# Routing of a two-layer encoder rebuilt: fewer serial steps, paced list scatters, gains loaded first, attention's projections spread over eight steps

## The chip, the cores and the metric

The kernel runs on one core of a Trainium2 chip. The metric is the device time of one execution in microseconds. A core has five engines with queues of their own: TensorE (PE, its weight loads shown as PEld), VectorE (DVE), ScalarE (ACT), GpSimd (POOL) and SyncE (SP, here only for transfers). Semaphores order them.

## The reference, cut to what matters

```python
# x: 1024 tokens x 1024, float32
h = x
h = h + mixer_ab(rmsnorm(h, g1), ...)       # layer 0: A: 9-chunk attention, 8 heads; B: window attention with sinks
h = h + dense_swiglu(rmsnorm(h, g2), ...)   # 1024 -> 2816 -> 1024
h = h + mixer_c(rmsnorm(h, g1), ...)        # layer 1: gated spatial mixing
h = h + moe_swiglu(rmsnorm(h, g2), ...)
return rmsnorm(h, final_norm)

def moe_swiglu(h, w_router, w_gate_e, w_up_e, w_down_e):
    logits = (xt @ w_router).astype(jnp.float32)      # 8 experts
    top_val, top_idx = lax.top_k(logits, TOP_K)       # TOP_K = 2
    gates = jax.nn.softmax(top_val, axis=-1)
    ...                                               # tokens sorted by expert
    ys = lax.ragged_dot(jax.nn.silu(hg) * hu, w_down_e, sizes)   # 1024 -> 3584 -> 1024
    ys = ys * gates.reshape(-1)[order][:, None].astype(ys.dtype)
    out = jnp.zeros_like(xt).at[tok].add(ys)
```

## The kernel before, in words

**Products.** Every float32 product is made of three products of a high and a low part (`product`, L307 on, all recorded at L316). Weights come in units of 128 x 1024 (512 KB) through four buffers `wraw[0..3]`. SP sends them (`load_units`, L292) when the buffer's last split is done; ACT makes the high part (`hi_part`, L298), DVE the low part (`lo_part`, L302). PE counts finished units in `unit_used`, DVE finished splits in `lo_done`.

**Start** (`start_act`, `start_dve`, `values_pe`). ACT and DVE multiply the first half of x by the gains of the norm and split it; PE multiplies it by the first weights, unscaled, and meanwhile sums squares and spreads the norm's factor (`start_sums_pe` L365, `start_spread_pe` L387). The gains are loaded by POOL, behind its first small operations. PE's first work of all is a small product for the T5 bias table (L2192), which waits for three small loads; its reader `ext_dve` stands behind the second weight part.

**Attention** (`attend_pe`, `attend_act`, `attend_dve`): 4 pairs of heads x 8 tiles t of 128 tokens, 32 steps, software-pipelined by hand. A step of PE: transposes of the A probabilities, A scores of the next step, half of the slices of a half projection if there is one, A values, B transposes, B scores, the other slices, B values. Pair p's second halves (`LATER`) are at t = 0, 1, 2 (units QA, KA, QB), and the first halves of the next pair (`AHEAD`) at t = 4, 5, 6; steps 3 and 7 have none. A half projection is 8 slices of k into one bank; ACT and DVE copy it out (`half_act`, `half_dve`, L784, L789) at the end of the step.

**Routing** (`mix_out_pe`, `route_dve`, `route_pool`). After the last projection of layer 1, PE makes the logits (L1114) and turns the hidden rows (`rows_pe`, L1128), ACT scales and copies them (`row_act`, L1150, L1152), and sends each at once: 16 scaled rows to `xrow_d` and 16 plain ones to `hrow_d`. DVE takes the top 2, sums the assignments of the tiles one after the other (L1647), PE ranks them (L1095 to L1097), DVE finds the least-loaded expert (`least`, `first_ok`), then every token's slot, then 8 masks `mine` (L1700) of the tokens of the first list, which PE turns into indices (`list_pe`, L1135); then the gates and the table of items (`cand`, `items_ok`), with the indices `tokl0` in the middle (L1721). POOL gathers x of the first item by these indices (L1778) once every `xrow_d` write has landed, and then scatters 16 x 128 entries of (token, gate) into the lists `tok_d` (L1787), and clears three buffers.

**Items** (`by_width`, `item_pe`, ...): a list of up to 384 tokens of one expert, at the least width of `WIDTHS` that holds it. 28 gate units and 28 up units, then 28 units of the down product: 84 units, in quads. Here there are 8 items: 3 of width 240, 2 of 256, 2 of 288, 1 of 304. x is turned by `turn_x_pe` (L1839). Beside the first units of an item the rows finished by the item before are normalised (`norm_beside_act`, `norm_beside_dve`). PE, ACT and DVE read the number of items as soon as `items_ok` is there.

A few lines that set the order:

```python
            for c in range(2):
                load_units(sp, src_e(e0, 0, c), Q_MOE, c)          # SP: 4 parts of the first quad, behind first_ok
            ...
            pool.wait_ge(slots_ok, 1)
            pool.wait_ge(gates_ok, 2)
            for t in range(NT):
                for c in range(2):
                    pool.indirect_dma_start(tok_d[:], ...)          # 16 scatters, back to back
```

## Time and profile before

| | |
|---|---|
| median of 3 runs | 3593.17 us (3589.37 to 3595.44) |
| profiled execution | 3593.88 us, its span 3592.1 us |
| mean granted clock of PE | 0.992 |
| DVE, ACT, POOL busy | 50%, 43%, 6% of the span |
| attention (steps) | about 103 to 405 us |
| routing, from the last projection to the first item | 1520.7 to 1556.2 us |
| items | 1556 to 3571 us |

Times in rows are microseconds from the span's start. A row of a timeline has its start, the time from its start to its end, engine, line, operation, written and read names, count, and in brackets the idle time before it and what ended it. A granted clock of 1.00 is 2.4 GHz and 0.50 is 1.2 GHz.

### The profile page before, as it was taken

The numbers are of one execution on the slowest core, as the hardware profiler recorded it, in microseconds if no ns is written. First come the engines' busy times: TensorE is split into PE (matmuls) and PEld (weight loads), VectorE is DVE, ScalarE is ACT, GpSimd is POOL, SyncE is SP. The second block draws the span as 40 slices with busy tenths as digits, with TensorE's granted clock in tenths as the row PEclk, the third lists the DMA queues.
The fourth block names the chain that finished last, engine by engine and source line by source line (L and its number), as shares of the span: only waits on it lengthen the run. The fifth ranks groups of instructions, "written<-read, shape, count | busy, mean of one in ns | idle before, by whom it ended". The sixth has DMA issues, their size and how long they took to land. (4 is left out here: it accounts for less than half of the span.)

```text
span 3592.1 us, 71989 instructions
## 1 busy us (share of the span) xinstructions
PE 3508.3 (98%) x27356; PEld 3338.3 (93%) x27356; DVE 1808.7 (50%) x2607; ACT 1544.6 (43%) x2216; POOL 203.3 (6%) x207
## 2 busy tenths in 40 slices
PE   8999899999999999979999999999999999999997
PEld 7888799999999999879899898998999999999997
DVE  6455543333333554365565555555655545545544
ACT  4455433333333333355454554544544444434433
POOL 1000000000000000040010010100101000000100
PEclk9999999999999999989999999999999999999999
DMA  5111323333322322266565565755656545544543
GB/s 198 35 47 45 138 94 97 96 97 118 97 96 94 123 88 97 81 209 205 186 236 194 193 230 186 234 194 196 228 187 205 182 158 181 191 164 155 183 160 124
DMA packets 158043, 540.81 MB, mean 151 GB/s; under 512 B 23480, under 2 KB 23520, under 8 KB 157920
## 3 DMA queue, kind: packets, MB, share of 16 engines
q1 hardware_dynamic: 129440, 467.72, 39.3%
q0 software_dynamic: 23872, 62.99, 5.0%
q10 hardware_dynamic: 4608, 8.39, 0.6%
q8 instruction: 86, 1.41, 0.2%
q14 instruction: 37, 0.30, 0.0%
HBM read 515.54 MB, written 45.48 MB: 156 GB/s over the span
## 5 line engine op out<-in xcount | busy, mean ns | idle before, releaser
L302 DVE TENSOR_TENSOR wl<-wraw,wh 128x1024 fp32r<-128x1024 f32 x884 | 1082.4, 1225 | 1307.0 <-ACT wh L298 1303.5
L298 ACT ACTIVATE wh<-wraw 128x1024 fp32r<-128x1024 f32 x884 | 934.3, 1058 | 1128.5 <-PE ps L316 1123.0
L316 PE MATMUL ps<-exh,wh 128*128 128x240 f32 (+3 forms) x3588 | 1018.0, 284 | 5.3 <-issue 5.2
L316 PE MATMUL ps<-exl,wh 128*128 128x240 f32 (+3 forms) x3584 | 1017.5, 284 | 1.5 <-issue 1.5
L316 PE MATMUL ps<-exh,wl 128*128 128x240 f32 (+3 forms) x3584 | 1017.2, 284 | 1.5 <-issue 1.4
L316 PE MATMUL ps<-xs,wh 128*128 128x256 f32 x5248 | 819.4, 278 | 2.4 <-DVE qAl L789 2.0
L316 PEld LDWEIGHTS ps<-xs,wh 128*128 128x128 f32 x5248 | 696.5, 188 | 12.5 <-issue 8.5
L316 PEld LDWEIGHTS ps<-exh,wh 128*128 128x128 f32 x3588 | 676.3, 189 | 8.0 <-issue 7.8
L316 PEld LDWEIGHTS ps<-exh,wl 128*128 128x128 f32 x3584 | 675.8, 189 | 1.6 <-issue 1.6
L316 PEld LDWEIGHTS ps<-exl,wh 128*128 128x128 f32 x3584 | 675.8, 189 | 1.6 <-issue 1.4
L316 PE MATMUL ps<-xs,wl 128*128 128x256 f32 x2624 | 512.8, 277 | 0.0
L316 PEld LDWEIGHTS ps<-xs,wl 128*128 128x128 f32 x2624 | 396.6, 188 | 0.0
L316 PE MATMUL ps<-wh,mah 128*128 128x512 f32 (+1 forms) x560 | 221.6, 396 | 0.0
L316 PE MATMUL ps<-wh,mal 128*128 128x512 f32 (+1 forms) x560 | 221.1, 395 | 0.0
L316 PE MATMUL ps<-wl,mah 128*128 128x512 f32 (+1 forms) x560 | 219.6, 392 | 0.0
L1288 ACT ACTIVATE mst<-ps 128x240 f32<-128x240 f32 (+3 forms) x224 | 87.5, 391 | 304.9 <-PE ps L316 230.4
L316 PE MATMUL ps<-mah,wh 128*128 (+2 forms) x672 | 200.3, 298 | 1.0 <-DVE exl L1850 1.0
L316 PE MATMUL ps<-mah,wl 128*128 (+2 forms) x672 | 200.0, 298 | 0.0
L316 PE MATMUL ps<-mal,wh 128*128 (+2 forms) x672 | 200.0, 298 | 0.0
L316 PE MATMUL ps<-ah,wh 128*128 (+2 forms) x704 | 138.3, 278 | 0.0
L316 PE MATMUL ps<-al,wh 128*128 (+1 forms) x704 | 138.1, 278 | 0.0
L316 PE MATMUL ps<-ah,wl 128*128 (+1 forms) x704 | 137.6, 277 | 0.0
(325 smaller groups left out, 3523.2 us busy)
## 6 DMA issues: line engine op xcount, KB each, us to landing
wraw<-in_w_expert SPq DMA_DIRECT2D x676, 512.0 KB
wraw<-in_w_main SPq DMA_DIRECT2D x208, 512.0 KB
hT<-in_xT POOLq DMA_DIRECT2D x2, 2048.0 KB, 9.7
h_d<-hT POOLq DMA_DIRECT2D x2, 2048.0 KB, 10.0
hT<-h_d POOLq DMA_DIRECT2D x2, 2048.0 KB, 13.7
xrow_d<-rows ACTq DMA_DIRECT2D x16, 256.0 KB, 2.0
hrow_d<-rows ACTq DMA_DIRECT2D x16, 256.0 KB, 3.4
yraw<-y_d POOLq DMA_DIRECT2D x4, 768.0 KB, 7.8
```

The costliest lines, as they stand in the source:

```text
L298: act.activation(wh[:, j], wraw[:, j], ACT.Copy).then_inc(hi_done, 1)
L302: dve.tensor_tensor(wl[:, j], wraw[:, j], wh[:, j].bitcast(F32), ALU.subtract).then_inc(lo_done, 1)
L316: mm = pe.matmul(out[:, s], a, b[:, s], start=first and part == 0 and c == 0, stop=last and part == 2 and d == n)
L1288: act.activation(buf[:, par, 0:n], bank(b + par, n), ACT.Silu).then_inc(silu_done, 1)
```

## The change

- **Start:** SP sends the gains ahead of everything. The T5 product goes behind the second slice of the value products, `ext_dve` behind the fourth weight part. The counters of the raw halves are joined with those of the scaled ones.
- **Attention:** a half projection is cut into pieces of 2 to 4 slices, two per step, over all eight steps from t = 3 of one pair to t = 2 of the next; the first pair keeps its halves at t = 0 to 2. At t = 0 (pairs 1 to 3) and t = 4 (pairs 0 to 2) the copies come early in the step.
- **Routing:** no serial sum over tiles: PE adds eight shifted bf16 products. The masks come from the rank among the least-loaded expert alone, ahead of the slots; the slots and gates are computed after the turn of x (`slots_dve`). The item table is smaller (13 items in place of 24). ACT copies a row before it sends the previous one, and only the first 8 plain rows and all scaled rows are sent by ACT; the last 8 plain rows stay in SBUF and POOL sends them one per unit of the first item (`last_rows_pool`); DVE waits for them (`rows_out`) behind the first twelve units. The 16 scatters wait for units 12, 14, ... 42 of the first item. POOL's clears and the final gains come ahead of them. The logits of the second half run one unit earlier. The first quad's part 0 is loaded behind `first_ok`, parts 1 to 3 only when x of the first item has arrived, and split after the turn.
- **Items:** the squares beside an item move two units back. The count of items is read by ACT and DVE after the last item.

```diff
+        THIRDS = ((QA, range(0, 3)), (QA, range(3, 6)), (QA, range(6, 8)), (KA, range(0, 3)),
+                  (KA, range(3, 6)), (KA, range(6, 8)), (QB, range(0, 4)), (QB, range(4, 8)))
+            if p == 0 and t < 3:
+                return (0, 1, *HALVES[2 * t + place])
+            if t < 3:
+                return (p, 1, *THIRDS[2 * t + 2 + place])
+            if p + 1 == PAIRS_A:
+                return None
+            if t < 7:
+                return (p + 1, 0, *THIRDS[2 * (t - 3) + place])
+            return (p + 1, 1, *THIRDS[place])
...
+            if 0 in ks:
+                pe.wait_ge(lo_done, unit_of(p, which) + 1)
+                pe.wait_ge(pj_lo, halves_before(p, half, which))
...
+        def early(p, t):
+
+            return (t == 0 and p >= 1) or (t == 4 and p + 1 < PAIRS_A)
...
+            pe.matmul(bank(SMALL, n, RANK), belowb[:], sentb[:], start=True, stop=False)
+            for back in range(1, NT + 1):
+                m = n - back * NE
+                mm = pe.matmul(bank(SMALL, m, RANK + back * NE), onesb[:], sentb[:, 0:m], start=False, stop=back == NT)
...
+        def last_rows_pool(pool):
+
+            pool.wait_ge(row_cp, 32)
+            for e in range(8):
+                t, b = 4 + e // 2, e % 2
+                pool.wait_ge(unit_used, 4 * Q_MOE + e + 1)
+                pool.dma_start(hrow_d[t * P:t * P + P, 512 * b:512 * b + 512], rows[:, e]).then_inc(last_st, 16)
...
+                    pool.wait_ge(unit_used, 4 * Q_MOE + 12 + 2 * (2 * t + c))
                     pool.indirect_dma_start(tok_d[:], bass.IndirectOffsetOnAxis(ap=slot[:, c, t:t + 1], axis=0),
                                             entry[:, c, t], None).then_inc(tok_st, 16)
...
-            for c in range(2):
-                load_units(sp, src_e(e0, 0, c), Q_MOE, c)
+            for j in range(4):
+                if j == 1:
+                    sp.wait_ge(x_got, 48)
+                sp.wait_ge(lo_done, 4 * Q_MOE + j - 3)
+                sp.dma_start(wraw[:, j], src_e(e0, 0, j // 2)[:, j % 2]).then_inc(raw[j], 16)
...
             turn_x_act(act, 0, XB0)
+            for j in range(1, 4):
+                hi_part(act, Q_MOE, j)
+            gap_exp_act(act)
+            act.wait_ge(items_ok, 1)
...
+            lo_part(dve, Q_MOE, 0)
             turn_x_dve(dve, 0, XB0)
+            for j in range(1, 4):
+                lo_part(dve, Q_MOE, j)
+            slots_dve(dve, own)
+            dve.wait_ge(items_ok, 1)
```

## Rows read from the trace of the kernel before

**Rows 1.** Part 1 of the page: busy us, share of the span, instructions

```profile
PE 3508.3 (98%) x27356; PEld 3338.3 (93%) x27356; DVE 1808.7 (50%) x2607; ACT 1544.6 (43%) x2216; POOL 203.3 (6%) x207
```

**Rows 2.** Waits of PE over the span: us in total, times, longest us

```profile
PE ps L2192 <- DMA onehot<-in_onehot: 10.8, 1, 10.8
...
PE ps L316 <- issue: 8.1, 14, 1.1
```

**Rows 3.** Stretch of the first 5 us: busy us and instructions by engine, clock, DMA share, GB/s

```profile
0.00:5.00 5.00, 0.00 (x0) 0.00 (x0) 0.00 (x0) 1.49 (x2) 3.78 (x13) 1.00 0.57 195
```

**Rows 4.** Timeline of the start: start us, us, engine, line, operation, idle time before and its releaser

```profile
8.04 1.33 ACT L335 ACTIVATE rsh<-yT,gains 128x512 fp32r<-128x512 f32 x2 [5.55 <-DMA gains<-in_gains]
...
12.15 0.80 PE L316 MATMUL ps<-wh,rsh 128*128 128x512 f32 x1
...
30.11 0.88 DVE L381 TENSOR_SCALAR dg<-ident,vstat 128x128 f32<-128x128 f32 x4
...
31.41 1.06 PE L387 MATMUL ps<-dg,ones 128*128 128x128 f32 x8
```

**Rows 5.** Timeline of DVE in attention: the copies of the finished B outputs

```profile
134.26 0.29 DVE L963 COPY ystB<-ps 128x128 f32<-128x128 f32 x1 [2.30 <-PE ps L763]
...
141.49 0.28 DVE L963 COPY ystB<-ps 128x128 f32<-128x128 f32 x1
...
152.58 0.29 DVE L963 COPY ystB<-ps 128x128 f32<-128x128 f32 x1 [2.53 <-PE ps L763]
...
175.62 0.29 DVE L963 COPY ystB<-ps 128x128 f32<-128x128 f32 x1 [2.43 <-PE ps L763]
...
181.44 0.29 DVE L963 COPY ystB<-ps 128x128 f32<-128x128 f32 x1
```

**Rows 6.** Timeline from the ranks to the first item's first product

```profile
1528.67 0.43 PE L1095 MATMUL ps<-sent,below 128*128 128x64 f32 x2 [1.11 <-DVE before L1647]
...
1529.54 0.17 DVE L1669 COPY place<-ps 128x8 f32<-128x8 f32 x1 [0.44 <-PE ps L1097]
...
1532.52 0.69 ACT L1150 ACTIVATE rows<-ps,rstd_t 128x512 f32<-128x512 f32 x1 [0.46 <-ACT rows L1150]
...
1535.89 2.73 DVE L1700 TENSOR_SCALAR mine<-range_c,lowest 128x384 bf16<-128x384 f32 x8
...
1540.30 0.16 DVE L1721 SCALAR_TENSOR_TENSOR tokl<-firstf 128x3 uint32<-128x3 f32 x1
...
1542.14 1.08 POOL L1778 DMA_INDIRECT xg<-xrow_d,tokl  x1 [17.84 <-DMA xrow_d<-rows]
...
1544.84 1.43 POOL L1778 DMA_INDIRECT xg<-xrow_d,tokl  x1 [0.30 <-issue]
...
1551.47 4.46 PE L1839 MATMUL ps<-ident,xg 128*128 128x128 f32 x24 [9.05 <-DMA xg<-xrow_d,tokl]
...
1556.22 0.37 PE L316 MATMUL ps<-exh,wh 128*128 128x240 f32 x1 [0.28 <-issue]
```

**Rows 7.** Part 5 of the page: DVE's split of a weight part

```profile
L302 DVE TENSOR_TENSOR wl<-wraw,wh 128x1024 fp32r<-128x1024 f32 x884 | 1082.4, 1225 | 1307.0 <-ACT wh L298 1303.5
```

**Rows 8.** Two stretches of 5 us in the first item, columns as in rows 3

```profile
1560.00:1565.00 5.00, 2.15 (x11) 1.36 (x9) 0.00 (x0) 0.00 (x0) 3.78 (x5) 1.00 0.02 1
...
1565.00:1570.00 5.00, 2.33 (x8) 1.69 (x8) 0.00 (x0) 0.00 (x0) 3.78 (x4) 0.51 0.02 1
```

**Rows 9.** Timeline: the last scatter, ACT's first and the later items' first Silu

```profile
1570.00 0.97 POOL L1787 DMA_INDIRECT tok_d<-entry,slot  x1 [0.30 <-issue]
...
1573.48 1.28 ACT L1288 ACT_TABLE_LOAD   x1 [16.54 <-remote]
...
1804.58 1.28 ACT L1288 ACT_TABLE_LOAD   x1 [1.63 <-PE ps L316]
...
2036.10 1.28 ACT L1288 ACT_TABLE_LOAD   x1 [1.63 <-PE ps L316]
```

**Rows 10.** Timeline of ACT behind the last item

```profile
3574.91 1.28 ACT L2223 ACT_TABLE_LOAD   x1 [2.27 <-issue]
```

More of the change, by code:

```diff
@@ L607, in values_pe @@
                             mm.then_inc((v_mm, unit_used)[g], 1)
+                        if g == 0 and k == 1:
+                            pe.wait_ge(setup_in, 48)
+                            pe.matmul(bank(6)[0:8, 0:EXT_B], t5s[:], onehot[:], start=True, stop=True).then_inc(t5_mm, 1)
                         if g == 0 and k == 4:
@@ L1092, in mix_out_pe @@
                 if e == 5:
-                    pe.wait_ge(sent_ok, 1)
-                    pe.wait_ge(t_root, 2)
-                    pe.matmul(bank(SMALL, NT * NE, RANK), below[:], sent[:].rearrange("p t e -> p (t e)"), start=True, stop=False)
-                    pe.matmul(bank(SMALL, NT * NE, RANK), ones[:], before[:, 0:NT].rearrange("p t e -> p (t e)"), start=False, stop=True)
-                    pe.matmul(bank(SMALL, NE, COUNT), ones[:], before[:, NT], start=True, stop=True).then_inc(rk_mm, 1)
+                    ranks_pe(pe)
             for e in range(8):
-                if e == 4:
+                if e == 6:
                     list_pe(pe)
@@ L1643, in route_dve @@
             own(last)
+            dve.tensor_tensor(sentb[:, 0:NT * NE], pick[:, 0].rearrange("p t e -> p (t e)"), pick[:, 1].rearrange("p t e -> p (t e)"),
+                              ALU.add).then_inc(sent_ok, 1)
             dve.tensor_tensor(sent[:], pick[:, 0], pick[:, 1], ALU.add)
-            own(dve.memset(before[:, 0], 0.0))
-            for t in range(NT):
-                last = dve.tensor_tensor(before[:, t + 1], before[:, t], sent[:, t], ALU.add)
-                if t < NT - 1:
-                    own(last)
-            last.then_inc(sent_ok, 1)
-            own(dve.tensor_copy(tokb[:].rearrange("p t a -> p (t a)"), tokf[:].rearrange("p t a -> p (t a)")))
             own(dve.tensor_tensor(gt[:, 0], top8[:, :, 1], top8[:, :, 0], ALU.subtract))
@@ L1656, in route_dve @@
             dve.wait_ge(rk_mm, 1)
-            count, more, rest, key, base_r, base_f, shift, room = (place0[:, v] for v in range(8))
+            more, rest, nkey, only, base_r, base_f, shift, room = (place0[:, v] for v in range(8))
             smaller = placed[:, 0]
+            count = bank(SMALL, NE, COUNT)
+            rank = bank(SMALL, NT * NE, RANK).rearrange("p (t e) -> p t e", e=NE)
             def over_e(v):
@@ L1667, in over_t @@
                 return v.rearrange("p (a e) -> p a e", a=1).to_broadcast([P, NT, NE])
-            rank = bank(SMALL, NT * NE, RANK).rearrange("p (t e) -> p t e", e=NE)
-            own(dve.tensor_copy(count, bank(SMALL, NE, COUNT)))
             own(dve.tensor_scalar(more, count, float(CAP), None, ALU.is_gt))
@@ L1673, in route_dve @@
             own(dve.scalar_tensor_tensor(rest, more, float(-CAP), count, ALU.mult, ALU.add))
-            own(dve.scalar_tensor_tensor(key, rest, float(NE), iota8[:, 0], ALU.mult, ALU.add))
-            own(dve.tensor_scalar(room, rest, 0.0, float(CAP), ALU.is_gt, ALU.mult))
+            dve.scalar_tensor_tensor(nkey, rest, float(-NE), iota8[:, 0], ALU.mult, ALU.subtract)
             own(dve.tensor_scalar(late[:, 0], rest, 0.0, -1e6, ALU.is_le, ALU.mult))
-            own(dve.scalar_tensor_tensor(late[:, 1], key, -1.0, late[:, 0], ALU.mult, ALU.add))
+            own(dve.tensor_tensor(late[:, 1], nkey, late[:, 0], ALU.add))
             own(dve.max(best8[:], late[:, 1]))
             dve.max_index(least[:], best8[:], late[:, 1]).then_inc(first_ok, 1)
-            own(dve.tensor_tensor(smaller, over_f(key), over_e(key), ALU.is_lt))
+            dve.scalar_tensor_tensor(val[:], rank, 1.0, sent[:], ALU.add, ALU.mult)
+            own(dve.tensor_scalar(only, late[:, 1], best8[:, 0:1], None, ALU.is_equal))
+            own(dve.tensor_tensor(placed[:, 1], val[:], over_t(only), ALU.mult))
+            own(dve.tensor_reduce(lowest[:], placed[:, 1], AX.X, ALU.add))
+            for t in range(NT):
+                dve.tensor_scalar(mine[:, t], range_c[:], lowest[:, t:t + 1], None, ALU.is_equal).then_inc(mine_ok, 1)
+            dve.wait_ge(list_mm, 1)
+            own(dve.tensor_scalar(firstf[:].rearrange("p s a -> p (s a)"), bank(LOGIT1, 2 * CAP // P, LIST), float(NT), None, ALU.add))
+            dve.scalar_tensor_tensor(tokl0[:], firstf[:, :, 0], float(P), firstf[:, :, 1], ALU.mult, ALU.add).then_inc(list_ok, 1)
+            dve.tensor_scalar(room, rest, 0.0, float(CAP), ALU.is_gt, ALU.mult)
+            own(dve.tensor_tensor(smaller, over_f(nkey), over_e(nkey), ALU.is_gt))
             own(dve.tensor_tensor(smaller, smaller, over_f(room), ALU.mult))
```

273 lines of the change are left out of this document (146 added, 127 removed).

## The prediction

> **What bounds the kernel now.** I first read the busy table of the page: TensorE (PE) is busy 98% of the span, so only its gaps and what crowds it can be won [rows 1]. The profiled execution took 3593.88 us, its span 3592.1 us with 1.8 us around it, and it is 0.7 us above the median of 3593.17; all sums below run against 3593.9. Next the list of what PE waited for: a first load, a first load for 10.8 us and "issue" for 8.1 us stand out [rows 2]. "Issue" is the one to look at twice, because it understates what happened: in the first item PE also crawled between these waits. Then the timelines of the start, of attention and of the routing.
>
> **Start: gains first, t5 product and its consumer later.** ACT's first operation sat 5.55 us waiting for `gains`, and PE's first product followed at 12.15 [rows 4]. Sent first on SP's queue, the 16 KB are there before x and the first weights; ACT then waits for x's first half MB, behind one more issue. At 195 GB/s in the first 5 us [rows 3] x and weights, 1 MB, are there after about 5 us, so ACT starts near 4.6 and PE could begin 3.4 us earlier. It can't keep that. Among the products of the first half stand those that spread the norm of x's second half: the diagonal they need was finished at 30.11 + 0.88 = 30.99, and PE asked for it at 31.41 [rows 4]. PE has therefore 0.4 us of slack there, and the squares behind the diagonal start with the landing of a load that is queued behind 4 MB and comes no earlier. I take 0.5 us gained; the bounds are 0 and 3.4. SP's queue starts x one issue (about 0.5 us) later, which is inside that bound. The t5 product goes past four weight products; its reader on DVE moves two weight parts later, and the tables built from it are used only after 95 us: nothing.
>
> **Attention: half projections over eight steps.** One step of DVE's copies of the finished B output to the next is one step of the loop. The steps without a projection are t = 3 (134.26 to 141.49, 7.2 us) and t = 7 (175.62 to 181.44, 5.8 us) [rows 5]. A half projection is 48 products of 256 columns; the neighbour t = 4 took 11.1 us with one in it [rows 5], and at 0.1125 us a product (the spacing within a projection) that is 5.4 us, leaving 5.7 for the step itself. Step t = 3 has one key tile less, so some 5.4 us of PE work, and 1.8 us of it was waiting; t = 7 has the small scores of the next pair, some 4.4 us of work, and 1.4 us of waiting. Both come three times (pairs 0 to 2; in pair 3 the late steps stay bare as before). Recoverable: 3 x 1.8 + 3 x 1.4 = 9.6 us. The work moved there (six of eight slices each) is only moved. Against it: at t = 4 and t = 0 the second unit starts in the middle of a step, in the same bank, and must wait for DVE's copy, which waits for ACT's, which stands behind two exponentials. Scores end + 2.9 us for the exponentials, + 0.6 and 0.7 for the copies is 4.2 us; PE comes back after two slices (1.35), the value products, transposes and B scores (2.4), 3.8 us: a stall of about 0.5 us six times, of which the old four waits of 0.5 us for the same copy pay part. I take 1.5 us, so 8.1 us gained; bounds 4 (each new place costs 1 us) and 9.6.
>
> **Routing, up to the first item's first product.** Step by step from [rows 6]. The rank product waited 1.11 us for the serial sums over the tiles; these become eight more small bf16 products, and one logit product less stands behind the last unit (0.5 us), so ranks start at 1527.1 and DVE's next part at about 1527.8 instead of 1529.54. From there to the `mine` masks DVE took 6.35 us; eleven dependent small operations of 0.20 to 0.25 us are left ahead of them: 2.4 us, masks from 1530.2, done 1532.9. The list product now stands behind six row transposes, the sixth of which needs all eight scaled copies; these took 1.15 us each with 0.46 us of waiting for themselves, and with the send held back one copy they take about 1.0: last copy 1532.8, list product done about 1534.7, list about 1535.3 against 1540.46. The gather also needs every xrow write landed: the last one goes at about 1533.4 and lands at 1536, so the gather starts at 1536.2 against 1542.14. In the trace it took until 1551.47, 9.3 us, of which three issues are 4.1 us and 5.2 us are landing behind four weight loads and the hrow writes. The change holds three of those four loads until x has arrived and gives all last hrow writes to POOL: I take 6.5 us, x at 1542.7. Turning x took 4.75 us to the first product and stays: 1547.5 against 1556.22, **8.7 us** gained. Bounds: 6.5 (gather 2 us slower) and 10.
>
> What is late next: weight parts 1 to 3 are sent at 1542.8 and split only after the turn. ACT 1549.2, DVE 1550.4, and PE wants part 1 at 1550.2; a DVE split is 1.23 us [rows 7]. Then ACT has two more parts, the exponential with its table, and the branch into the item; the first Silu comes at about 1556, DVE's split of the next quad at 1559 behind the slot arithmetic (14 operations, 3.5 us), PE wants it at 1558.3. Each is small, together **1.5 us** lost; bounds 0 and 4. The hrow writes: eight, one per unit of 2.7 us, the last allowed at unit 8 (1569), and DVE waits for them only at the twelfth (1580): free; it would take over 1 us more per write to cost anything. The x gather of item 1 and hg need the list at unit 70; the last scatter goes at unit 42, leaving 28 units or 75 us: free.
>
> **The scatters.** This is the largest term. Sixteen ran back to back until 1570.97. PE flowed for 4 us from 1556.22 and then had 11 and 8 products in two stretches of 5 us, where some 45 fit at the full clock of the first and 23 at the half clock of the second [rows 8]; ACT, with its item code just ahead, stood 16.5 us until 1573.48, 2.5 us after the last scatter [rows 9], when PE flowed again. I read it as both waiting for their next instructions behind the scatters. The price is exact by comparing items: from first Silu of item 1 to that of item 2 is 231.5 us [rows 9], and the wait before item 1's Silu ended at about 1804.4, so without a loss unit 0 of item 0 would stand 231.5 us before that, at 1572.9, but it started at 1556.22 and takes 2.7, so it ended at 1558.9: item 0 took **14.0 us** longer than item 1. With one scatter every two units, from unit 12, PE is in a loop that it has already read, and no two queue up. In the old trace eight scatters passed from 1547.8 to 1560.2 while PE turned x and did its first products, with no such crawl. I take the 14.0 whole; bounds 0 and 14.
>
> The Trainium skill (Runtime: NRT & Kernel Launch, Instruction fetch mechanics) says a taken branch out of the prefetched window forces a fetch by DMA before execution can go on. By that alone the crawl belongs to the entry into the item, would stay, and the sum would be 14 us smaller.
>
> **The end.** ACT now loads the item count after the last item, ahead of the table load of the final norm, which stood 2.27 us behind loop exit and four such loads and width tests [rows 10]. One load more is about 0.5 us on the last chain; bounds 0 and 1.
>
> **Sum:** -0.5 - 8.1 - 8.7 + 1.5 - 14.0 + 0.5 = -29.3, so 3593.9 - 29.3 = **3564.6 us**.
>
> **Rivals.** (1) *The crawl stays*, because it comes with the cold branch and not with the scatters. For it: it sits at the entry, and ACT stands longest exactly there. Against: PE's waits for "issue" are 8.1 us in all [rows 2], nearly all of them here, though the other width changes branch too; and it ended with the scatters. It gives 3578.6. Chance 0.12. The skill's branch rule is this one.
> (2) *Attention gives nothing*: the shorter slices (two or three in place of four) no longer cover the softmax chain in steps t = 0, 1, 4, 5, so what t = 3 and 7 win is lost there. From scores to scaled probabilities is about 4.1 us, and PE has 6.4 us of other work in between, which speaks against it. 3572.7. Chance 0.12.
> (3) *Each paced scatter stalls PE by itself* (the slower side). From 1560.2 to 1570.97 about eight scatters cost some 8.7 us, 1.0 each, and the last had a tail of 2.4 us. If a loop must be read again each time round, sixteen lone scatters cost 3.4 each: 54 us, and 3564.6 + 54 = 3619. It turns slower from 29.3/16 = 1.8 us a scatter. Against it: the eight harmless ones, and the 8 items' gathers and scatters of rows, which left no wait for "issue". Chance 0.06.
> (4) *The routing gain is eaten*: the row writes, the late weights or the gates hold the first item, and the 8.7 us vanish (the crawl still goes). 3573.3. Chance 0.10.
>
> **Numbers.** The forecast holds 0.60. All but (3) are faster by far over 0.2% (7.2 us, about what a measurement here can tell from no change); a half of (3), and 0.02 for mixtures of (1), (2) and (4), could come near zero. Faster 0.91, same 0.03, slower 0.06. The terms' bounds reach from -3.4 - 9.6 - 10 - 14 = -37 (3557) to about -20 (3574); I add (1) at 3578.6, which gives 3556 to 3579.
>
> **What would show it.** Right: ACT begins near 4.5 us but the spread products come no more than 1 us earlier; t = 3 and t = 7 steps of about 9.5 us with no wait for ptA; the gather at about 1536 minus what the stages before have won (8.6), first product at 1539 in the trace's own time, and the first Silus of items 0 and 1 just 231 us apart. Wrong: "issue" waits on PE during units 12 to 42, an ACT gap over 4 us before the first Silu, DVE standing at the wait for the row writes, or waits on qAl or kAl above 1 us each.

## The result, and the profile after

The changed kernel took 3572.02 us (median of 4 runs, 3569.05 to 3572.61) against 3592.41 (3589.37 to 3595.44, 4 runs): ratio 0.9948, interval 0.9936 to 0.9960. A second set of runs of the same two kernels gave 3570.15 (3568.16 to 3573.24, 4 runs) against 3590.01 (19 runs). The first set's profiled execution has a span of 3570.6 us, 21.5 less than the one before.

The start and the spread of the norm, from the timeline of the changed kernel [rows 4]:

```profile
5.31 1.33 ACT L341 ACTIVATE rsh<-yT,gains 128x512 fp32r<-128x512 f32 x2 [2.82 <-DMA yT<-in_xT]
...
9.23 0.76 PE L322 MATMUL ps<-wh,rsh 128*128 128x512 f32 x1 [9.23 <-DVE wl L308]
...
29.14 0.88 DVE L387 TENSOR_SCALAR dg<-ident,vstat 128x128 f32<-128x128 f32 x4
...
30.16 1.02 PE L393 MATMUL ps<-dg,ones 128*128 128x128 f32 x7 [0.63 <-DVE dg L387]
```

ACT begins 2.7 us earlier (at 5.31, forecast 4.6) and PE 2.9, and the spread products, which wait for their diagonal now, 1.25: the pinch is where it was expected.

In attention the copies of the finished B output mark the steps [rows 5]:

```profile
144.09 0.29 DVE L1007 COPY ystB<-ps 128x128 f32<-128x128 f32 x1 [1.73 <-PE ps L792]
...
174.71 0.29 DVE L1007 COPY ystB<-ps 128x128 f32<-128x128 f32 x1 [2.52 <-PE ps L792]
183.98 0.29 DVE L1007 COPY ystB<-ps 128x128 f32<-128x128 f32 x1 [1.99 <-PE ps L792]
190.76 0.29 DVE L1007 COPY ystB<-ps 128x128 f32<-128x128 f32 x1 [1.19 <-PE ps L792]
198.22 0.29 DVE L1007 COPY ystB<-ps 128x128 f32<-128x128 f32 x1 [1.14 <-PE ps L792]
...
218.09 0.29 DVE L1007 COPY ystB<-ps 128x128 f32<-128x128 f32 x1 [1.75 <-PE ps L792]
```

Step t = 7 lasts 9.27 us with work in it (5.82 bare, before), t = 0 6.78 (8.44), t = 1 7.46 (10.05). A whole pair, from the end of one t = 3 to the next (144.09 to 218.09), takes 74.00 us; before it took 75.92 (141.49 to 217.41).

Routing, from the rank product to the first item's first product [rows 6]:

```profile
1525.00 0.20 PE L1174 MATMUL ps<-sentb,belowb 128*128 128x72 bf16 x1
...
1527.76 2.73 DVE L1752 TENSOR_SCALAR mine<-range_c,lowest 128x384 bf16<-128x384 f32 x8
...
1531.00 0.16 DVE L1755 SCALAR_TENSOR_TENSOR tokl<-firstf 128x3 uint32<-128x3 f32 x1
...
1534.46 1.08 POOL L1849 DMA_INDIRECT xg<-xrow_d,tokl  x1 [12.12 <-DMA xrow_d<-rows]
...
1537.38 0.99 POOL L1849 DMA_INDIRECT xg<-xrow_d,tokl  x1 [0.30 <-issue]
...
1541.47 4.78 PE L1913 MATMUL ps<-ident,xg 128*128 128x128 f32 x24 [9.77 <-DMA xg<-xrow_d,tokl]
...
1546.00 0.36 PE L322 MATMUL ps<-exh,wh 128*128 128x240 f32 x1
```

From the ranks to the masks 2.8 us pass (7.2 before), from the masks' start to the list 3.2 (4.4); the list is there 3.5 us before the gather starts, so the gather waits for nothing but the row writes (before, the list was there only 1.7 us ahead of it). It is turned 4.1 us after its last issue began (6.6 before).

The first item, and the table load of the final norm at the end [rows 9, 10], from ACT's timeline:

```profile
1551.48 1.28 ACT L1362 ACT_TABLE_LOAD   x1
...
1781.55 1.28 ACT L1362 ACT_TABLE_LOAD   x1 [1.63 <-PE ps L322]
...
2013.07 1.28 ACT L1362 ACT_TABLE_LOAD   x1 [1.63 <-PE ps L322]
...
3553.58 1.28 ACT L2295 ACT_TABLE_LOAD   x1 [4.39 <-issue]
```

ACT no longer stands 16.5 us. From the first product of item 0 to the load of item 1 are 235.55 us (248.36 before), and to the load of item 2 another 231.52. The load at the end stands 4.39 us, 2.1 more than before.

By these marks the 21.5 us are: 2.0 to the end of the last projection before the logits, 8.3 in the routing up to the first product, 12.8 in the first item, 0.4 in the other items and 0.2 behind the load, less 2.1 at the load; that makes 21.6, with 0.1 of rounding. So start and attention, forecast at 8.6 together, gave 2.0 here. The windows of the last pair of heads show one cause (busy time and count of PE, PEld, DVE, ACT and POOL, granted clock, DMA share, GB/s):

```profile
360.00:365.00 5.00, 3.52 (x26) 2.53 (x26) 4.11 (x9) 2.68 (x6) 0.00 (x0) 0.61 0.99 382
365.00:370.00 5.00, 4.96 (x31) 4.30 (x33) 2.55 (x10) 2.33 (x5) 0.00 (x0) 0.50 1.02 399
370.00:375.00 5.00, 5.00 (x39) 4.08 (x36) 3.05 (x8) 2.33 (x5) 0.00 (x0) 0.53 0.13 52
```

The granted clock is at its lower level, 1.2 GHz, for some 13.6 us of these 15 (an estimate from the three means); the profile of the kernel before has 1.00 in the same three windows, though other profiles of the old layout have a fall there too (b_clears 0.80 and 0.51 from 365 to 375 us).

### The profile page after: what moved, and what is told of

The parts are those of the page before. It is cut to its first block and busy times, and to the rows that moved or that the text cites. A ratio compares the mean times of both kernels' runs of the same rounds, so it can differ in the third digit from the quotient of the medians.

```text
span 3570.6 us, 71995 instructions
## 1 busy us (share of the span) xinstructions
PE 3506.5 (98%) x27359; PEld 3338.1 (93%) x27359; DVE 1807.0 (51%) x2601; ACT 1543.9 (43%) x2216; POOL 202.6 (6%) x214
```

## Experiments

Twelve runs follow, in three sets, two of them the kernels before and after once more; each set has its own runs of the kernel before (medians 3589.85, 3590.01 and 3590.82 us). Most single executions of one kernel lie within 3 to 4 us of its median, a few up to 8.6 us above it, and the 95% interval of a ratio reaches 3 to 6 us to either side, so traces and medians are both given; each trace is one execution. Three intervals are read off each trace, all between events that every version has:

- A: first copy of ystB to the last, the whole of attention;
- B: last copy of ystB to the first product of item 0, so the rest of the mixer and the routing;
- C: that product to item 1's table load on ACT, so item 0. An item takes 231.5 us from load to load, and item 0's load stands one unit of 2.7 us behind its first product, so without a loss C is 234.2.

| version | time, us | runs | A | B | C |
|---|---|---|---|---|---|
| before | 3592.41 | 4 | 290.57 | 1151.77 | 248.36 |
| b_again (before) | 3589.23 | 10 | 289.92 | 1149.61 | 242.71 |
| b_paced | 3585.79 | 10 | 290.81 | 1154.42 | 234.56 |
| b_burst | 3585.72 | 10 | 291.15 | 1153.36 | 236.31 |
| b_clears | 3581.59 | 10 | 290.64 | 1151.20 | 234.57 |
| b_hg | 3584.96 | 11 | 290.81 | 1151.50 | 236.08 |
| after | 3572.02 | 4 | 287.31 | 1144.60 | 235.55 |
| a_again (after) | 3570.15 | 4 | 283.85 | 1143.66 | 237.15 |
| a_no_attn | 3576.68 | 5 | 290.57 | 1145.95 | 235.48 |
| a_no_start | 3571.15 | 4 | 284.31 | 1145.26 | 235.30 |
| a_no_route | 3572.88 | 5 | 283.35 | 1151.70 | 236.34 |
| a_load | 3570.32 | 4 | 285.05 | 1145.57 | 235.53 |
| a_weights | 3572.94 | 5 | 284.03 | 1146.17 | 235.41 |
| a_warm_load | 3570.04 | 5 | 288.77 | 1142.15 | 234.87 |

### The scatters alone, paced or in one burst

**b_paced** is the kernel before with the changed kernel's order on POOL for this part: clears and final gains ahead, each scatter behind its unit.

```diff
+            pool.memset(hg[:], 0.0).then_inc(hg_z, 1)
+            pool.memset(xg[:], 0.0).then_inc(hg_z, 1)
...
             for t in range(NT):
                 for c in range(2):
+                    pool.wait_ge(unit_used, 4 * Q_MOE + 12 + 2 * (2 * t + c))
                     pool.indirect_dma_start(tok_d[:], ...
```

> The kernel before, with one thing of the change alone: the 16 list scatters wait for units 12, 14, ... 42 of the first item (the clears and the final gains have to move ahead of them). Theory A (the scatters hold up the instruction fetch of PE and ACT at the entry of the item): item 0 takes as long as item 1, no issue wait on PE in it, 14 us less than before, about 3579 us. Theory B (the crawl belongs to the cold branch into the item): it stays, 3593 us. Theory C (each lone scatter costs PE by itself): over 3593 us, with issue waits during units 12 to 42.

Measured: 3585.79 us (3582.49 to 3594.34), ratio 0.9989 (0.9980 to 0.9999); its profiled span 3583.2.

**b_burst** waits for unit 12 once and then sends all sixteen back to back.

```diff
+                    if t == 0 and c == 0:
+                        pool.wait_ge(unit_used, 4 * Q_MOE + 12)
```

> As b_paced, but only the first scatter waits, for unit 12; the other 15 follow back to back, as in the kernel before, while PE, ACT and DVE are in their loops. Theory A, narrow form (only code that is not yet in the engine is held up, a loop that runs is immune): the same 3579 us as b_paced, no issue waits. Theory A, wide form (back-to-back scatters slow any code, loops too): the crawl of about 14 us comes back at units 12 to 20, about 3593 us.

Measured: 3585.72 us (3582.39 to 3590.66), ratio 0.9991 (0.9981 to 1.0000); span 3583.3.

Both take the first item (C) from 248.4 to 234.6 and 236.3 us, as theory A has it, and yet each gained only 4 us by the medians, hardly clear of nothing by the intervals. The pacing itself matters little: the times are the same, and a burst inside the loop has a C 1.7 us longer than lone scatters, in one profile each. What else happened is in the timeline of b_paced, DVE first and then POOL:

```profile
1548.93 6.66 DVE L1740 CAST itab<-itf 1x25 int32<-1x25 f32 x1
```

```profile
1547.52 1.45 POOL L1778 DMA_INDIRECT xg<-xrow_d,tokl  x1 [0.30 <-issue]
1548.96 1.40 POOL L1782 MEMSET ybuf<- 128x1536 f32 x1
1550.28 2.68 POOL L1783 MEMSET hg<- 128x3072 f32 x1
1552.88 2.68 POOL L1784 MEMSET xg<- 128x3072 f32 x1
```

The last operation of the item table, 25 numbers, is on record for 6.66 us. It ends at 1555.59, and the third clear on POOL at 1555.56. In b_burst the two are 1553.92 and 1553.89. PE begins to turn x 1.02 us after the table in both, though the gather had landed by then (5.6 to 6.7 us from issue to landing; the last one was issued at 1547.52 in b_paced): my own order of the clears had put a new wait ahead of the item.

### The clears held back until the table is stored

**b_clears** is b_paced with one line more.

```diff
             pool.memset(ybuf[:], 0.0).then_inc(y_z, 1)
+            pool.wait_ge(items_ok, 1)
             pool.memset(hg[:], 0.0).then_inc(hg_z, 1)
```

> b_paced with one wait more: POOL's clears of hg and xg don't start before the item table is stored. In b_paced that table's last CAST on DVE was held for 6.66 us beside those clears (1.46 us in the kernel before), and the first item's turn began 1.0 us after it, at 1556.61, 9.1 us after the last gather's issue (6.6 before). Theory: the clears on POOL held DVE back, and so the table; with the wait the cast takes about 1.5 us again, the turn begins 6.6 us or less behind the last gather's issue, and the kernel is 2 to 3 us faster than b_paced: 3583.3. Rival: the gather landed late by itself (9.1 us again) and the time stays at 3585.8.

Measured: 3581.59 us (3577.63 to 3589.08), ratio 0.9981 (0.9971 to 0.9990). In its trace:

```profile
1547.51 0.66 DVE L1740 CAST itab<-itf 1x25 int32<-1x25 f32 x1
1547.60 4.61 DVE L302 TENSOR_TENSOR wl<-wraw,wh 128x1024 fp32r<-128x1024 f32 x4
```

The table is stored in time, the turn begins 6.8 us after the last gather's issue, and the kernel is 4.2 us faster than b_paced. Against the kernel before in its own set it is 8.4 us faster by the medians (3.6 to 10.4 by the interval). That is what this part of the change is worth to a typical run; the prediction had 14.0.

### The kernel before a second time

> The kernel before itself, for a second profiled execution. In the first one the end of attention's last step (the last copy of ystB) stood at 404.45 us, the first item's first product at 1556.22, the second item's table load on ACT at 1804.58 (248.4 after it, against 231.5 for the item behind), the span was 3592.1. If the crawl of the first item is the program's (theory), those 248.4 us come again within 1 us. If its size is chance, they differ by several us. The copy at 404.45 may move by 2 or 3 us if the falls of TensorE's clock move.

Measured: 3589.23 us (3586.83 to 3592.27). C is 242.71, not 248.36: the expectation missed, and the difference shows where the time goes. ACT and POOL of this second execution, in two fences:

```profile
1559.74 1.28 ACT L1288 ACT_TABLE_LOAD   x1 [2.24 <-PE ps L316]
...
1575.15 1.06 ACT L1945 ACTIVATE on<-hg 128x1024 f32<-128x1024 f32 x1 [10.79 <-POOL hg L1790]
```

```profile
1571.31 0.97 POOL L1787 DMA_INDIRECT tok_d<-entry,slot  x1 [0.30 <-issue]
1572.28 2.68 POOL L1790 MEMSET hg<- 128x3072 f32 x1
```

and PE's windows:

```profile
1560.00:1565.00 5.00, 5.00 (x46) 5.00 (x45) 2.62 (x4) 3.81 (x5) 3.78 (x5) 1.00 0.04 2
1565.00:1570.00 5.00, 5.00 (x46) 5.00 (x45) 0.38 (x2) 0.00 (x0) 3.81 (x4) 1.00 0.64 209
```

Nine scatters were issued in these 10 us and PE did 46 products in each window, the full rate; in the first profile it did 11 and 8 [rows 8]. ACT came to its first Silu without delay and then stood 10.79 us at the square of an hg row, which waits for the clear of hg. POOL does that clear behind the sixteen scatters. Weight parts stand behind ACT, and PE ran dry for 5.73 us at 1573. So there is a plain wait in the kernel before, hidden in the first profile behind the crawl.

One record bears on the crawl itself. A block of instructions (16 KB, the profile's queue `q8 instruction`) was fetched in each profile near the entry into the item. It took 2.74 us from 1558.93 in the first profile, the longest fetch in all fourteen traces (the median of that profile's 136 is 0.93), and 1.81 in b_again; in b_hg, also beside scatters, it took 0.93. But the long one had ended at 1561.67, and PE went on crawling until about 1573.4, 2.4 us behind the last scatter's issue. The profile does not say for which engine. A slow fetch stands at the head of the crawl, then, but what kept it going isn't shown.

### Clears first, scatters at once and unpaced

**b_hg** takes that wait away and leaves the scatters' run where it was.

```diff
+            pool.wait_ge(items_ok, 1)
+            pool.memset(hg[:], 0.0).then_inc(hg_z, 1)
+            pool.memset(xg[:], 0.0).then_inc(hg_z, 1)
+            pool.wait_ge(hg_z, 2)
             pool.wait_ge(slots_ok, 1)
...
-            pool.wait_ge(tr_mm, 24)
-            pool.memset(hg[:], 0.0).then_inc(hg_z, 1)
-            pool.memset(xg[:], 0.0).then_inc(hg_z, 1)
-            pool.wait_ge(hg_z, 2)
             pool.wait_ge(tok_st, 16 * 2 * NT)
```

> The kernel before with POOL's clears of hg and xg ahead of the sixteen scatters (behind the item table), and the scatters at once and back to back as before, not paced. Theory W: what held the first item was ACT's wait for the clear of hg, which stood on POOL behind the scatters (10.79 us in the second profile of the kernel before); then nearly all of the gain of pacing (8.4 us, 3581.6) comes here too: 3581 to 3583.5, no wait of ACT over 3 us between 1556 and 1580, first product to the second item's table load 234 to 237 us. Theory C, the one of the prediction: the scatters' run itself holds up the engines; then ACT or PE stands again until the last scatter, that stretch is 242 to 248 us, and the time is 3588 to 3592.

Measured: 3584.96 us (3581.61 to 3592.99, 11 runs), ratio 0.9986 (0.9977 to 0.9995), 5.9 below its own runs of before. C is 236.08. PE's windows, with four to five scatters in each:

```profile
1560.00:1565.00 5.00, 5.00 (x47) 5.00 (x46) 0.90 (x2) 3.21 (x4) 3.78 (x5) 1.00 0.10 30
1565.00:1570.00 5.00, 5.00 (x47) 5.00 (x46) 3.74 (x6) 4.25 (x9) 4.09 (x4) 1.00 0.55 167
1570.00:1575.00 5.00, 5.00 (x47) 5.00 (x46) 2.95 (x4) 3.60 (x6) 3.80 (x4) 1.00 0.86 188
```

Theory W holds: with every scatter in its old place at the entry into the item, the order of the clear gives 5.9 us by the medians (1.8 to 8.3 by the interval). The time is 1.5 us above the window given. The 2.5 us between 5.9 and the 8.4 of b_clears are inside the intervals; in the traces C differs by 1.5. And most of that 1.5 is one more wait for something queued behind the scatters. POOL sends the final gains behind them here, and DVE stood for these gains:

```profile
1591.74 0.18 DVE L1955 RECIPROCAL fstat<-fstat 128x3 f32<-128x3 f32 x1 [5.74 <-DMA fgb<-in_final_norm]
```

```profile
1590.00:1595.00 5.00, 4.39 (x39) 4.20 (x38) 3.22 (x6) 1.28 (x3) 0.00 (x0) 1.00 0.28 110
1595.00:1600.00 5.00, 5.00 (x43) 4.86 (x44) 5.00 (x8) 2.01 (x5) 0.17 (x1) 1.00 0.57 180
```

PE then ran dry for 0.61 us and did 10 to 12 products fewer than the 46 or 47 that the windows around have, an estimated 1.1 to 1.3 us at 0.11 us a product. That leaves next to nothing for the scatters themselves.

### The changed kernel a second time

> The changed kernel itself, for a second profiled execution. Theory A (the bare steps of the last pair leave TensorE so idle that the clock falls there each time): granted clock near 0.5 again for about 15 us somewhere in 355 to 380 us and again at 395 to 410, last copy of ystB at 401.4 within 1 us. Rival (where the falls come is chance, as the version with the old start, which has none at 355 to 380, suggests): the falls are elsewhere and the last copy comes at 397 to 400.

Measured: 3570.15 us (3568.16 to 3573.24). The fall of the clock between 360 and 375 us is gone:

```profile
360.00:365.00 5.00, 2.66 (x29) 1.84 (x26) 4.11 (x12) 2.37 (x6) 0.00 (x0) 1.00 1.01 394
365.00:370.00 5.00, 4.76 (x56) 3.71 (x53) 2.98 (x11) 3.86 (x10) 0.00 (x0) 1.00 0.88 344
370.00:375.00 5.00, 3.53 (x38) 2.65 (x38) 4.14 (x13) 3.71 (x8) 0.00 (x0) 1.00 0.01 3
```

and A is 283.85, 3.5 us shorter than in the first profile. Theory A falls in the form given: that fall was one execution's. Only one late in the pair, between 390 and 405 us, came in every profile of the new layout that has no added work there; the old one has one there too, mostly five to ten us later.

### Attention and start undone, one at a time

**a_no_attn** puts the half projections back on six steps.

```diff
-            if p == 0 and t < 3:
-                return (0, 1, *HALVES[2 * t + place])
-            if t < 3:
-                return (p, 1, *THIRDS[2 * t + 2 + place])
...
+            ks = range(4 * place, 4 * place + 4)
+            if t in LATER:
+                return (p, 1, LATER[t], ks)
+            if t in AHEAD and p + 1 < PAIRS_A:
+                return (p + 1, 0, AHEAD[t], ks)
+            return None
...
-            return (t == 0 and p >= 1) or (t == 4 and p + 1 < PAIRS_A)
+            return False
```

> The changed kernel (3572 us) with attention's half projections put back to steps 0 to 2 and 4 to 6 in halves, the copies at the ends of the steps. Theory A (the new spread wins 1.8 us per pair, 5.5 in all, but in this kernel the granted clock falls to half in the bare steps of the last pair, which costs 3.7 us): 5.5 us of steps are lost, and if the clock stays full in the last pair as it did before, 3.7 come back: about 3574 us. Theory B (the spread pays as much as its waits, 8 us, and the loss is elsewhere): 3580 us. The clock of 360 to 375 us tells whether the fall belongs to the spread (full here) or not (half here too).

Measured: 3576.68 us (3574.01 to 3578.09), ratio 0.9960 (0.9946 to 0.9975). The eight runs of the changed kernel have their median at 3571.9, so the layout is worth 4.8 us, and no run of the one reaches into the range of the other. The clock doesn't settle whose the fall is: it was full from 360 to 370 us here and 0.66 from 370 to 375. A agrees: seven profiles with the old layout have 289.9 to 291.2 (mean 290.6), six with the new one and no added products 283.4 to 287.3 (mean 284.7), 6.0 apart.

**a_no_start** sends the gains behind POOL's constants, and does the t5 product first, as before.

```diff
-            sp.dma_start(gains[:], io["gains"]).then_inc(gain_in, 16)
...
+            pool.dma_start(gains[:], io["gains"]).then_inc(gain_in, 16)
             pool.dma_start(relr[:], io["rel_rev"]).then_inc(setup_in, 16)
```

> The changed kernel with its start put back (gains by POOL, T5 product first, its reader behind the second weight part). Theory A (the earlier start wins 1.2 us at 34 us and loses it to a fall of the clock at 105 to 110 us): PE starts at 12.15 again, attention begins at the same 114 us, 3572 us within 2. Theory B (the start is worth its 1.2 us and the clock's falls do not depend on it): 3573.2 us, with the same falls.

Measured: 3571.15 us (3567.66 to 3573.54), no difference from 3571.9 that these runs can tell. The first copy of ystB, the nearest mark behind the start, stands at 112.6 to 113.0 us in three profiles of the new start without a fall of the clock ahead of it, and at 113.88 in the one of the old start that has none; with falls it stands up to 117.1 in the old and 116.0 in the new. About 1 us, then, by one profile on the old side.

### The routing undone

**a_no_route** is b_clears with the new start and the new attention layout, so the changed kernel with the routing, row writes and item table of before. Of its diff against the changed kernel, the ranks on PE:

```diff
-            for e in range(8):
-                if e >= 6:
-                    pe.wait_ge(row_cp, 16 + e - 5)
...
-                if e == 5:
-                    ranks_pe(pe)
...
+                    pe.wait_ge(sent_ok, 1)
+                    pe.wait_ge(t_root, 2)
+                    pe.matmul(bank(SMALL, NT * NE, RANK), below[:], ...
```

> The changed kernel with the old routing: the kernel before with the new start, the new places of attention's products, the clears ahead and the scatters paced. From the traces: last projection to the first item's first product 35.5 us again (27.2 with the new routing), 8.3 more, and ACT's wait ahead of the last table load 2.27 us rather than 4.4, 2.1 less, the first item 1 us shorter. So 5 us slower than the changed kernel's 3571: 3576, and 5.5 us faster than the 3581.6 of the version with the clears and the paced scatters alone. Rival: the new routing's gain is given back in the first item and at the end; then this is within 2 us of 3571.

Measured: 3572.88 us (3571.07 to 3577.66, 5 runs), ratio 0.9950 (0.9937 to 0.9964). The traces say what was expected: B is 1151.70 (five profiles with the old routing have 1149.6 to 1151.8, mean 1151.2, leaving out b_paced and b_burst, whose table was held) against 1143.7 to 1146.0 (mean 1145.0) in the five with the new one and the weights held back, a_warm_load aside. And the load at the end

```profile
3554.10 1.28 ACT L2256 ACT_TABLE_LOAD   x1 [2.44 <-issue]
```

stands 2 us less. Compared with a_again, which has nearly the same A and start, the span is 4.8 us longer (3571.1 against 3566.3). But the medians are only 1.0 us apart, with five and eight runs, which is what the rival has. The routing's net gain is thus between 1 and 5 us, and these runs don't say where.

### The end: item count read before the loops

**a_load**:

```diff
-            by_width(act, lambda it, n: item_act(act, it, n))
             n_items = act.value_load(nitem[0:1, 0:1], min_val=1, max_val=NIT)
+            by_width(act, lambda it, n: item_act(act, it, n))
```

> The changed kernel with ACT reading the number of items ahead of the three loops rather than behind them. In the profile of the changed kernel ACT stood 4.39 us at the end ahead of its table load with nothing to wait for (2.27 before). If the read itself, cold behind the loops, is what costs, the wait falls to about 2.3 us or less and the time to 3570.0 (2 us below the changed kernel). If it is the extra branches of the loops by width, the wait stays at 4.4 us and the time at 3572.

Measured: 3570.32 us (3568.04 to 3572.62), and

```profile
3553.22 1.28 ACT L2295 ACT_TABLE_LOAD   x1 [3.42 <-issue]
```

The wait falls by 1.0 (3.00 in a_warm_load, 1.4 less), not by 2.1. The read behind the loops is a half to two thirds of it; the rest lies in something else between the last loop's exit and the load, and stays open.

### Weights no longer held back for the gather

**a_weights**:

```diff
             for j in range(4):
-                if j == 1:
-                    sp.wait_ge(x_got, 48)
                 sp.wait_ge(lo_done, 4 * Q_MOE + j - 3)
```

> The changed kernel without SP's wait for the gather ahead of parts 1 to 3 of the first quad of weights. Theory: the gather of 128x1024 rows lands 4.1 us after its last issue because nothing else is on the DMA engines (6.6 in the kernel before, where the weights run beside it); without the wait it lands 1.5 to 2.5 us later, PE's wait for it is 11 to 12 us rather than 9.8, the 0.4 us of PE's wait for the second unit's low part goes, and the time is 1 to 2 us longer: 3572 to 3573. Rival: the queues don't share, the landing stays at 4.1 us, and the time falls by 0.4 us.

Measured: 3572.94 us (3569.73 to 3575.05). Rows for the gather and the turn:

```profile
1533.40 1.30 POOL L1849 DMA_INDIRECT xg<-xrow_d,tokl  x1 [0.30 <-issue]
```

```profile
1538.21 5.35 PE L1913 MATMUL ps<-ident,xg 128*128 128x128 f32 x24 [11.39 <-DMA xg<-xrow_d,tokl]
```

4.81 us from the last issue to the turn, against 3.8 to 4.3 in the six other profiles with the new routing, and B, 1146.17, is just above the 1143.7 to 1146.0 of the others. Holding the weights back is worth 0.5 to 1 us, less than expected: most of the way from the 6.6 of before (5.2 to 6.8 in the profiles with the old routing whose table was in time) to 4.1 has another cause, and the change's other step there, the hrow writes moved behind the gather, wasn't tried by itself. The time, 1 us above 3571.9, fits but could not show it alone.

### TensorE kept busy in the last pair

**a_warm_load** is a_load with eight unused products of 128 columns in each place of the last pair that has no piece; what is computed for the output is the same.

```diff
             if piece is None:
+                pe.wait_ge(pj_lo, halves_before(PAIRS_A - 1, 1, QB) + 1)
+                for _ in range(8):
+                    pe.matmul(bank(PJ, P), ident[:], ident[:], start=True, stop=True)
                 return
```

> The changed kernel with eight products of ident by ident more in each free place of the last pair of heads (places that have no projection products left; their results are not used), and ACT reading the number of items ahead of the loops. Theory: the falls of TensorE's granted clock between 355 and 410 us come because TensorE idles in the bare steps there; with it kept busy they go, and last minus first copy of ystB is 283.5 us or less (287.3, 283.9, 285.1, 284.3 in four profiles of the new layout), the time 3568 to 3570. Rival: the falls come all the same, or the eight products lie on the path of the steps (ptA is what a bare step waits for, up to 3.1 us): 3571 to 3574.

Measured: 3570.04 us (3569.35 to 3576.00). PE's windows where the last fall had stood in every other profile, a_again first and a_warm_load second:

```profile
395.00:400.00 5.00, 4.49 (x25) 4.16 (x26) 3.33 (x6) 3.48 (x6) 0.00 (x0) 0.53 0.02 3
```

```profile
395.00:400.00 5.00, 5.00 (x57) 4.59 (x57) 3.25 (x6) 3.53 (x5) 0.00 (x0) 1.00 0.01 3
400.00:405.00 5.00, 5.00 (x51) 4.54 (x48) 1.91 (x4) 3.62 (x6) 0.00 (x0) 1.00 0.00 0
```

Both halves of the expectation came true at once. The clock stays at 2.4 GHz from 355 to 415 us, and B, at whose head the late fall costs, is the shortest of all, 1142.15. But the products also lie on the steps' path: A is 288.77, 4.9 us above a_again's. The two cancel; fewer products a place might leave a gain, which wasn't tried.

None of the twelve beats the changed kernel by more than its runs differ among themselves.

## Why the prediction was right or wrong, point by point

**The total.** 3564.6 was forecast, 3572.0 measured, inside 3556 to 3579, and faster as given. The sum of -29.3 was 8 us too large: -21.3 in the profiled executions.

**Start, -0.5.** Right in kind: ACT's wait went and the spread products became the next thing late, 1.25 us earlier than before. By the first copy of ystB about 1 us is left of it, twice the term, and nothing that a median shows.

**Attention, -8.1.** Right in kind, too large: 5.5 in three clean pairs (1.9 and 1.8 each), 6.0 by A, 4.8 by a_no_attn. Rival (2), nothing gained, is out. The step that failed is the price of t = 7: "some 4.4 us of work, and 1.4 us of waiting". With six slices of 0.675 us in it the step took 9.27, so 5.2 of its own, and it took up 0.6 us, not 1.4: 3 x 0.8 = 2.4 us short. For t = 3 the same sum gives 9.62 - 4.05 = 5.57, against 5.4 forecast: 1.66 taken up, 1.8 forecast. The stalls were sized well: over the other steps of a pair, 0.4 us a pair net. In the two profiles shown, the changed kernel is 6.7 us ahead at the end of t = 3 of the last pair (366.48 against 373.18; 1.4 us of this is luck, one step of the kernel before that took 12.46 us at 229.87 and 11.1 everywhere else), and only 2.0 at the end of the last projection. The rest was given back to two stretches at the lower clock (360 to 375 and 395 to 405 us) in the last pair, where the new layout's bare steps are what they were before. The prediction priced the moved work, and nothing for what TensorE's clock does; one execution's fall there was worth 3.5 us (A of the two profiles of the changed kernel), more than the step's error of 2.4.

**Routing up to the first product, -8.7.** The best term: 8.3 from the end of the last projection in the two profiles shown, 6.1 as the mean of B over all of them. Corrected for the 2.0 us won ahead of it, the gather began at 1536.4 (forecast 1536.2), though the list was there 2.2 us earlier than forecast, and the turn came 7.0 us later (forecast 6.5). The weights beside the gather are a small part of its landing (a_weights).

**Late weights and the rest, +1.5.** PE waited 0.43 us for the second unit's low part in the profile shown, and 0.2 or nothing in the others. C is 235.3 to 235.6 in five profiles, 237.15 in one and 234.87 in a_warm_load, so 0.7 to 3.0 above the 234.2 without a loss. But without this part of the change it is 234.57 in b_clears and 236.34 in a_no_route. So the term lies inside its bounds of 0 and 4, and its size isn't shown. The row writes on POOL, one per unit until 1569.04, held nothing, and rival (4) in this form is out. Whether the routing's gain comes through to the end as a whole is not settled: the traces say 4 to 5 us net, the medians 1.

**The scatters, -14.0.** The size was near for this profile (12.8 in C, with the term before it), by the luck of which execution was profiled, and the mechanism is what failed: "I read it as both waiting for their next instructions behind the scatters". Two runs speak against it as the usual cause. In b_again PE kept its full rate beside nine scatters, and b_hg kept all sixteen at the entry and lost only 1.5 us of C against the paced one, most of it in DVE's wait for the final gains. The wait that the order of the kernel before builds in was ACT's for the clear of hg, which POOL does behind the scatters. The change moves that clear and the final gains ahead, which its description names and the prediction gives no term: it counted the scatters on POOL's queue and not who waits for what stands behind them. The part's worth is 8.4 us by medians (b_clears), of which 5.9 come with the clear's place. In the traces, one each, the 13.8 us between 248.36 and 234.57 are 5.65 of crawl, 6.6 with the clear (242.71 to 236.08) and 1.5 with the rest. The 5.65 us by which the first profile's item was longer than the second's are the crawl, and its cause stays open: no experiment reproduced it. The first profiled execution, 3593.88 us, lay 4 us above the 3589.9 of 20 later runs, and a term read exactly from one execution took all of the crawl into the forecast.

**Rival (1)**, the crawl stays because the branch is cold: with the scatters and the clear out of the way item 0 loses 0.4 to 3.0 us, not 14, and the branch is the same. As a forecast it is out; whether the cold branch had a part in the one crawl on record stays open, with its cause. By the Trainium skill (Runtime: NRT & Kernel Launch, Instruction fetch mechanics), a taken branch out of the prefetched window waits for a fetch; b_clears takes the same branches with PE at its full rate right behind the first products, so the rule alone would not have priced this.

**Rival (3)**, 1 to 3.4 us a paced scatter: out. With sixteen paced scatters b_paced has a C of 234.56, 0.4 above an item without loss, where the rival had at least 1 us a scatter, and b_burst has the same time.

**The end, +0.5.** Too small, and outside its bounds of 0 and 1: +2.1 in the profile shown and +1.9 in the second. The step that failed is taking one load as a quarter of the 2.27 us that the loop exit, four loads and the width tests share; by a_load and a_warm_load it is 1.0 to 1.4, and 0.7 to 1.1 of the 2.1 stays open.

**The terms together,** by medians: scatters and clears 8.4, attention 4.8, start 0 to 1, routing with the end 1 to 5. They make 14 to 19, where the medians of the two kernels are 20.4 apart in the first set and 19.9 in the second (14 to 25 by the second's interval).

## What to carry to other kernels

When a run of small transfers stands in the way on a queue, list what is queued behind it and who waits for that before pricing the transfers themselves: here two clears of 2.7 us each, moved ahead, were most of the gain, and a load of gains left behind cost most of what still lacked. Before a difference between two iterations is taken as a term to a tenth of a us, look at a second profiled execution; here the same item differed by 5.65 us. And a moved clear is not free either: put beside the last small operation of a table that all engines wait for, it cost 4 us. The changed kernel has no wait between the two either: its table is done ahead of the clears in six profiles of the seven with it, and in a_warm_load it was not.

## What the runs showed of the hardware

**A small cast on DVE ended only with POOL's run of clears.** Wherever the item table's last cast met POOL's clears, in eight profiles of eight, its record ends 0.03 or 0.04 us after the end of the last of the back-to-back clears: 1547.69 and 1547.66 (before), 1547.81 and 1547.77 (b_again), 1555.59 and 1555.56 (b_paced), 1553.92 and 1553.89 (b_burst), 1548.17 and 1548.13 (b_clears), 1551.11 and 1551.08 (b_hg), 1539.12 and 1539.09 (a_no_route), and 1543.30 and 1543.27 in a_warm_load, which has the changed kernel's table of 14 numbers. The other six profiles of that table have the cast ahead of the clears, and it takes 0.16 us there. In a_warm_load it took 5.90; PE turned x meanwhile, and its first product came 5.53 us behind the start of the turn, against 4.4 to 5.0 in the others.

Splits of a weight part, with two inputs in SBUF, ran at their usual 1.2 us beside the same clears in b_clears (four in 4.61 us), where the cast was already done. Behind a waiting cast they started at their usual spacing but ended only with it, here in b_paced (min, median and max in ns, first and last start):

```profile
L302 DVE TENSOR_TENSOR wl<-wraw,wh x4: 3168/4869/6572, 1549.0 to 1552.4; 128x1024 fp32r<-128x1024 f32 x4
```

The Trainium skill (SBUF — State Buffer, Who interferes with whom) says that a cast on VectorE can enter a mode that takes the ports shared with GpSimd, that whoever has them holds them for the whole instruction, and that a two-input operation contends only with a GpSimd operation that reads SBUF. The traces agree in that the cast waited and the splits of b_clears did not. Beyond it, the cast did not get in between three clears in a row (6.6 us in b_paced, 1548.96 to 1555.56). It was held too where its record begins ahead of the first clear, by 0.03 us in three profiles and by 0.55 in b_hg; POOL was at the issue of the last gather then, and whether that issue holds the ports isn't shown.

**TensorE's clock fell in different places in different executions of one program.** The changed kernel's 360 to 375 us were at 0.61, 0.50 and 0.53 in one and at 1.00 in the other; the stretch of the start, 95 to 115 us, had falls in nine of twelve experiments' profiles and moved the first copy of ystB between 112.6 and 117.1. What came every time, whatever the layout, was a fall at the end of the last pair's bare steps, behind windows in which PE was busy for some 2 to 3 of 5 us, and it went when PE was given work there.
